# A group's first products copied by ScalarE, and VectorE's residuals put one behind each of those products

## The reference

```python
x = layer_norm(DEEPNORM_ALPHA * x + g1 * mix, ln1_g, ln1_b)
h2 = x * (1.0 + sc2) + sh2
f = jnp.einsum("btf,fd->btd", jnp.square(jax.nn.relu(jnp.einsum("btd,df->btf", h2, w_up))), w_down)
x = layer_norm(DEEPNORM_ALPHA * x + g2 * f, ln2_g, ln2_b)
```

## Time and profile before

| | |
|---|---|
| median of 3 runs (lowest, highest) | 2214.82 us (2210.22 to 2215.65) |
| the profiled execution | 2205.87 us, its span 2204.2 us |
| mean granted TensorE clock | 0.986 |
| PE busy | 2110.0 us, 96% |
| DVE busy | 1513.3 us, 69% |
| POOL busy | 1461.9 us, 66% |
| ACT busy | 863.2 us, 39% |

### The profile page before, as it was taken

One profiled execution on the slowest core, in us unless ns is written; L12 is line 12 of the kernel. 1 busy time (PEld: TensorE's weight loads), 2 busy tenths in 40 slices (PEclk: granted clock), 3 DMA queues, 4 the chain that ended last, 5 costly groups with the idle time before them and its releaser, 6 DMA issues.

```text
span 2204.2 us, 27806 instructions
## 1 busy us (share of the span) xinstructions
PE 2110.0 (96%) x10342; PEld 1741.9 (79%) x10342; DVE 1513.3 (69%) x2055; ACT 863.2 (39%) x1173; POOL 1461.9 (66%) x1115
## 2 busy tenths in 40 slices
PE   7989999999989999999989999999999999999994
PEld 3556788788889788888868888877888889999983
DVE  1554479778687665567788757698857787665578
ACT  1200322323212355445544545644554554444440
POOL 4324578786424367787787778877878876666675
PEclk9999999999999999999999999999999999999997
DMA  8546588795333254454624564534564544444331
GB/s 265 159 153 219 200 240 254 211 279 178 113 105 116 86 187 146 159 185 135 200 94 145 177 217 144 173 111 143 182 212 145 168 121 125 146 166 151 116 125 43
DMA packets 324089, 357.78 MB, mean 162 GB/s; under 512 B 16280, under 2 KB 256105, under 8 KB 323954
## 3 DMA queue, kind: packets, MB, share of 16 engines
q1 hardware_dynamic: 323954, 355.99, 51.1%
HBM read 321.34 MB, written 34.59 MB: 161 GB/s over the span
## 4 chain that ended last, share of the span: by engine, by line
PE 64%; DVE 12%; issue 1%; ACT 1%; DVEq 0%; ACTq 0%
PE ps L1096 21%; PE ps L1097 20%; PE ps L1098 20%; PE ps L1361 1%; DVE xt L1922 1%; DVE hid_a L1880 1%; DVE pair_sums L1900 0%; DVE pair_sums L1899 0%; DVE pair_sums L1901 0%; DVE hid_b L1880 0%; PE ps L1430 0%; DVE mix L1541 0%; DVE more_sums L1985 0%; DVE acc L1990 0%; DVE htmp L1723 0%
## 5 line engine op out<-in xcount | busy, mean ns | idle before, releaser
L856 POOL TENSOR_TENSOR w_hilo<-w_raw,w_hilo 128x512 fp32r<-128x512 f32 x890 | 1279.5, 1467 | 692.5 <-ACT w_hilo L941 692.2
L941 ACT ACTIVATE w_hilo<-w_raw 128x1024 fp32r<-128x1024 f32 x445 | 470.6, 1059 | 712.8 <-PE ps L1098 606.4
L1096 PE MATMUL ps<-hA,w_hilo 128*128 128x512 f32 (+1 forms) x1760 | 622.2, 354 | 16.1 <-ACT htmp L992 8.0
L1097 PE MATMUL ps<-hA,w_hilo 128*128 128x512 f32 (+1 forms) x1760 | 620.8, 353 | 0.0
L1098 PE MATMUL ps<-hA,w_hilo 128*128 128x512 f32 (+1 forms) x1760 | 620.3, 352 | 0.0
L1096 PEld LDWEIGHTS ps<-hA,w_hilo 128*128 128x128 f32 x1760 | 332.2, 189 | 60.1 <-issue 15.4
L1097 PEld LDWEIGHTS ps<-hA,w_hilo 128*128 128x128 f32 x1760 | 332.2, 189 | 41.6
L1098 PEld LDWEIGHTS ps<-hA,w_hilo 128*128 128x128 f32 x1760 | 332.1, 189 | 41.7
L1972 DVE TENSOR_TENSOR acc<-acc,ps 128x512 f32<-128x512 f32 x270 | 178.4, 686 | 78.0 <-PE ps L1098 75.1
L1096 PE MATMUL ps<-w_hilo,hid_a 128*128 128x512 f32 x450 | 178.0, 396 | 7.3 <-DVE more_sums L1969 7.3
L1096 PE MATMUL ps<-w_hilo,hid_b 128*128 128x512 f32 x450 | 175.5, 390 | 3.5 <-POOL w_hilo L856 3.5
(11 more groups left out here) (233 smaller groups left out, 3014.9 us busy)
## 6 DMA issues: line engine op xcount, KB each, us to landing
w_raw<-in_w_up SPq DMA_DIRECT2D x128, 512.0 KB, 4.0
w_raw<-w_mix SPq DMA_DIRECT2D x124, 512.0 KB, 3.3
w_raw<-in_w_down SPq DMA_DIRECT2D x97, 512.0 KB, 3.6
w_raw<-in_w_in SPq DMA_DIRECT2D x64, 512.0 KB, 4.7
xt<-in_w_ada SPq DMA_DIRECT2D x22, 1024.0 KB
w_raw<-in_w_out SPq DMA_DIRECT2D x32, 512.0 KB, 5.0
xt<-x_norm SPq DMA_DIRECT2D x19, 512.0 KB, 5.7
xt<-in_w_down SPq DMA_DIRECT2D x36, 256.0 KB, 5.1
```

Source lines behind the costliest of these rows:

```text
L856: ins = pool.tensor_tensor(W[:, g % SLOTS, 1, cols], raw[:, g % RAW, cols], W[:, g % SLOTS, 0, cols], ALU.subtract)
L941: act.activation(W[:, g % SLOTS, 0, :], raw[:, g % RAW, :], ACT.Copy).then_inc(hi_done, 1)
L1096: pe.matmul(out, w_hi, x_hi, start=start, stop=False)
L1097: pe.matmul(out, w_hi, x_lo, start=False, stop=False)
```

## The change

ScalarE copies a group's seven first products into the places of the sums (`begin_sums`), in all four groups. For the groups behind the first it waits until the old contents are no longer needed: `sums_ready` for the places of products 0 to 2, and a new semaphore `x_added`, which each residual raises, for those of products 3 to 6. The copies stand ahead of the `hi_part` of the same product. VectorE copies nothing there any more. Its residuals of tiles 3, 2, 1, 0 stand behind K(b,0), K(b,1), K(b,2), K(b,3), one each. The statistics of tiles 3 and 2 stay behind K(b,4); those of tiles 1 and 0 and the inverse root move behind K(b,6).

```diff
+            def begin_sums(b, j):
+                s = b // BLOCKS
+                if s:
+                    act.wait_ge(d_evac, 2 * PRODUCTS * b)
+                    act.wait_ge(sums_ready, 2 * s - (1 if j < 2 else 0))
+                    if j > 2:
+                        act.wait_ge(x_added, 4 * s - (2 if j < 5 else 0))
+                for i in range(2):
+                    if i:
+                        act.wait_ge(slab_used, SLAB["K", b, j] + 1)
+                    else:
+                        act.wait_ge(d_done, PRODUCTS * b + j + 1)
+                    act.activation(sums_of[j](i), ps[:, product_bank(b, j, i), :], ACT.Copy).then_inc(d_evac, 1)
...
+                if kind == "K" and b % BLOCKS == 0:
+                    begin_sums(b, i)
...
-                do(dve.scalar_tensor_tensor(x, x, ALPHA, acc[0:r, t, :], ALU.mult, ALU.add))
+                signal(dve.scalar_tensor_tensor(x, x, ALPHA, acc[0:r, t, :], ALU.mult, ALU.add), x_added,
+                       4 * s + 4 - t)
...
-                    if b % BLOCKS == 0:
-                        dve.tensor_copy(a, src).then_inc(d_evac, 1)
-                    else:
-                        dve.wait_ge(d_evac, sums_done(b - 1, j, i))
-                        dve.tensor_tensor(a, a, src, ALU.add).then_inc(d_evac, 1)
+                    dve.wait_ge(d_evac, sums_done(b - 1, j, i))
+                    dve.tensor_tensor(a, a, src, ALU.add).then_inc(d_evac, 1)
...
-                elif i == 2:
-                    end_residual(s, 3)
-                    end_residual(s, 2)
...
-                if s and r == 1 and n == 0:
-                    for t in range(4):
+                if s and r == 1:
+                    for t in ((3, 2), (1, 0))[n]:
                         end_sums(t)
-                    sync()
-                    rsqrt(0, 4, ln_end)
+                    if n:
+                        sync()
+                        rsqrt(0, 4, ln_end)
...
-                else:
+                elif b % BLOCKS:
                     down(b, i)
...
-                if (kind, i) == ("K", 1) and s and r == 0:
-                    end_residual(s - 1, 1)
-                    end_residual(s - 1, 0)
+                if kind == "K" and i < 4 and s and r == 0:
+                    end_residual(s - 1, 3 - i)
```

More of the change, by code:

```diff
@@ L464, in decoder_layer_kernel @@
         acc_gated = sem("acc_gated")
+        x_added = sem("x_added")
         y_scaled = sem("y_scaled")
```

## The result

The changed kernel takes 2197.82 us (median of 4 runs, 2192.95 to 2199.85), the kernel before beside it 2214.28 (4 runs). The ratio is 0.9925, 95% interval 0.9904 to 0.9947. Timed again with more runs, it took 2194.3 against 2212.3 us, ratio 0.9918 (0.9904 to 0.9931). So the change is faster by 0.5 to 1.0%. The profiled execution took 2192.95 us, with a span of 2191.1 and a mean clock of 0.987.

The account below looks back on a forecast made before the run. PE, busy 96% of the span, bounds the kernel, so only its holes and slow-clock stretches can give time. Gains of 6.5 us in group 1 and 7.6 in group 2, 14.1 together, take 2214.8 to 2200.7 us; range 2193 to 2209.

Parts of the forecast that it names:

- No hole before U(9,2): Start of groups 1 and 2: earlier pair sums remove PE's 3.99 us wait and the slow clock behind it.
- the clock rival: New wait before K(8,3), K(16,3) also lowers the clock; 1.7 + 2.4 us come back, 2204.8 us; chance 0.17.
- The way from the pair sums to K(8,3): Group 1: from the end of (9, first pair)'s sums through ScalarE's copy to K(8,3)'s start, 4.8 us.
- When the pair sums of (9, first pair) end: VectorE, group 1: at 1137.4, with 0.97 us of GpSimd contention for each of three low parts.
- my 3.2: Predicted new PE wait before K(8,3) for ScalarE's copy of K(8,1), 3.2 us in place of 0.70.
- No wait behind it: After K(8,3): K(8,4) follows at once, later copy waits are covered and slab parts cost nothing.
- the likeliest case: The forecast itself: 2200.7 us, own range 2197 to 2204, chance 0.55.
- the rival of slab parts behind every copy: All 28 first products: PE waits 2 × 0.60 us each, losing 33.4 us, time 2234.1 us; chance 0.06.
- ScalarE waiting for a residual without PE: Copies of K(8,3) wait on ScalarE for two residuals until about 1145.7, covered to within a few tenths.
- ScalarE's busy time: Profile after the change: ScalarE 33 us busier, from 14 copies a group at 0.60 us.
- Groups 0 and 3 and the statistics at nothing: Copies in groups 0 and 3, and moving the statistics and inverse root of tiles 1 and 0, change nothing.
- The clock: Group 3's 3.24 us hole left the clock at 1.00, taken as evidence against the new 3.2 us hole lowering it.

Follow-up runs that it names:

- Experiment 3: Changed kernel with the residuals of tiles 3 and 2 put back behind U(8,2) and U(16,2): 2200.0 us, ratio 0.9952 to the kernel before.
- experiment 8: Both kernels profiled again, nothing edited: the kernel before took 2207.35, 2209.65 and 2213.6 us, the changed kernel 2195.73 us.
- Experiment 7: Changed kernel with K(8,4)'s slab high part early and ScalarE's copies of K(8,1), K(16,1) ahead of it: 2193.65 us, ratio 0.9915 to the kernel before.
- The third trace: Third profiled execution of the changed kernel, nothing edited: 2195.73 us.
- The second execution: Second profiled execution of the changed kernel, nothing edited; the kernel timed again had a median of 2194.3 us, ratio 0.9918 to the kernel before.
- experiment 6: Changed kernel with the high part of K(8,4)'s slab ahead of the pair sums' high parts, groups 1 and 2: 2193.67 us, ratio 0.992 to the kernel before.
- experiment 2: Changed kernel with residuals and statistics at their old places, so only the copies on ScalarE remain: 2201.91 us, ratio 0.9961 to the kernel before.
- experiment 4: Changed kernel with all statistics and the inverse root back behind K(8,4): 2197.39 us, ratio 0.9946 to the kernel before.
- experiment 5: Changed kernel with ScalarE copying in groups 1 and 2 only, VectorE in groups 0 and 3: 2197.03 us, ratio 0.9934 to the kernel before.

## Why the prediction was right, step by step

Predicted were 2200.7 us, 14.1 us less; measured were 2197.82 and 2194.3, with differences of 16.5 and 18.0.

**No hole before U(9,2): right.** I had the pair sums end 0.17 us after K(8,0)'s start (1125.6 against 1125.43) and found 0.18, and the clock is 1.00 behind it. Experiment 3 brings the hole back with the residuals alone. The clock behind the hole was no loss by itself, as experiment 8 shows; my sum did not count it, since it went by the start of K(8,4), but the clock rival took its price of 1.7 and 2.4 us from there.

**The way from the pair sums to K(8,3): right.** I took 4.8 us; it is 1139.67 − 1134.89 = 4.78 in group 1 and 4.77 in group 2. Experiment 7 removes that wait by taking the copies out of this chain.

**When the pair sums of (9, first pair) end: mis-sized by up to 1.4 us.** I took 11.8 us behind those before them, with 0.97 of contention for each of three low parts. It is 10.4 in group 1 and 11.6 in group 2. The first low part takes 2.29 or 2.30 in place of 1.23, the 128x512 one stays at 0.69, and the third is the one that varies. VectorE in group 2, and GpSimd there:

```profile
1462.13 1.57 DVE L1898 TENSOR_TENSOR hid_a<-htmp,hid_a 128x256 fp32r<-128x256 f32 x1
```

```profile
1462.12 8.47 POOL L857 TENSOR_TENSOR w_hilo<-w_raw,w_hilo 128x512 fp32r<-128x512 f32 x6 [1.83 <-ACT w_hilo L942]
```

Where GpSimd's slab part started 0.01 us ahead (1462.12), the low part took 1.57 us; where both started at 1128.72, it took 0.42. The third trace has the same pair, 1.57 and 0.42, and the hole before K(8,3) follows: 2.77 and 2.75, against 1.61 and 1.62. The second execution, for which I had expected one of these two sizes, shows a third in group 1: the part of `outputs` took 1.22 us, the sums before it ended 1.15 us earlier, and the three low parts took 2.29, 1.67 and 1.41, which is all of my contention; the hole is 2.43. So that hole has several sizes, 1.6 to 2.8 us, and none as long as my 3.2.

**No wait behind it: wrong.** I had costed the slab parts at nothing in the likeliest case and gave PE no hole before U(9,3). There is one of 0.63 to 0.99 us in each group where the clock stayed up. Its cause is not the rival of slab parts behind every copy (whose price of 28 × 1.20 is 33.6 us, not 33.4). It is the one `hi_part` behind the pair sums' high parts, and a GpSimd slowed beside the residuals; experiment 6, which moves that instruction, removes it. The limit is not new: the kernel before had it, hidden under the wait for the copies of K(8,2) (experiment 2). It takes back what K(8,3) gained on my figure. I had K(8,3) 16.8 us behind K(8,0), and it came 15.4 to 16.5 behind; I had 10.9 us from there to K(8,5), and it took 12.2 to 12.6. So that my K(8,5), 19.5 + 2.72 + 5.44 = 27.7 us behind K(8,0), is close to the six measured distances, 27.60 to 29.10, is partly luck: two errors of opposite sign.

**ScalarE waiting for a residual without PE: right.** It idled 2.43 us in group 1, and no hole of PE ends there. **ScalarE's busy time** rose by 26.2 us, not 33: two copies back to back take 1.06 us together.

**Groups 0 and 3 and the statistics at nothing: right** by the traces of experiments 4 and 5.

**The clock: read from one execution, and wrong as a rule.** I said that a hole of 3.24 us leaves the clock at 1.00. The same hole, released by the same instruction, stands in all fourteen profiled executions of the nine kernels, 3.23 or 3.24 us long. The way from its end to K(24,0) took 19.14 to 19.16 us in four, 20.47 to 20.71 in nine and 21.96 in one. So the clock rival was not excluded by the row that I set against it; it came true in one of six holes of the changed kernel, and cost 0.3 us there, not the 1.7 or 2.4 that I had set for it. Of the four that kept the clock three are of the kernel before, so the change may lose about 1.2 us there; why, is open. In return the hole before K(8,4), which I priced at its 2.7 us, cost 1.4 to 1.6 us of clock in five of eight places, and that goes too. The advice in the Trainium skill ("TensorE: Matmul & The Clock Gate", section "Why this matters for your kernels") against idle gaps agrees with this. Here the clock fell also behind gaps shorter than the one I had taken as safe and shorter than those of which the Trainium skill warns: 2.17 us in experiment 6.

**The sum.** By the mean distances the change is worth (35.6 + 36.0) − (28.4 + 28.4) = 14.8 us (three executions of the changed kernel), less 1.2 in group 3: 13.6. The mean spans differ by 2207.4 − 2194.3 = 13.1 us; the rest is 0.7 us by which the changed executions reach K(8,0) later on average, and 0.2 us less behind K(24,0). The timed difference of 18.0 has an interval of 15.3 to 21.2 us, so at least 1.7 us of it are not explained (the first timing's, 11.7 to 21.3, holds the 13.6). The executions differ by up to 6.3 us in when they reach K(8,0) (1123.79 to 1130.11). All of that lies ahead of the MLP, which the change leaves alone: from K(0,0) to K(8,0) is the same in each. Whether the unexplained rest is there stays open.

## What to carry to other kernels

When holes of the bottleneck engine are the target, take several profiled executions first: here one trace showed a hole of 3.99 us that is 2.85 in others, and a clock that held where it mostly falls. A stretch at the lower clock ahead of another wait may cost nothing, because the wait takes it up; price it by the start of the product behind that wait. A hole that is removed uncovers the one under it: here the supply of slabs, no later than before. Look for the one instruction of the supply chain that stands behind a wait, and put it ahead (experiments 6 and 7). A copy that another engine waits for should not stand behind a chain that waits for a third.

## What the runs showed of the hardware

**A tie between VectorE and GpSimd.** The same 128x256 low part takes 0.42 us or 1.57, and the same 128x1024 addition 1.22 or 2.35, and which it is goes by GpSimd's start. At the starts of groups 1 and 2 the fourteen traces, which hold the starts in ns, have 52 of these low parts and additions that begin within 0.03 us of an instruction with which GpSimd leaves an idle stretch. In 38 of them GpSimd's start lies 5 to 24 ns ahead, and VectorE's instruction took 1.1 us longer. In the other 14 it lies at most 4 ns ahead, or later than VectorE's, and VectorE's took no longer. The Trainium skill ("SBUF — State Buffer", section "SBUF: two separate sides") describes the pair of ports that they share as an exclusive lock, which whoever starts first holds for the whole instruction. The traces agree but for those 4 ns, and some 0.01 us decided over 1.15 us of PE's time.

**The clock behind equal holes.** Holes of 2.85 us in one execution left the clock at 1.00 and at 0.78; holes of 2.43 to 2.78 us left it at 1.00 in five places of the changed kernel and experiment 5, at 0.76 in three of the changed kernel and experiment 4; behind holes of 3.97 to 3.99 us the next 24 matmuls took 1.4 us or more longer in all seven places with one. The shortest hole of groups 1 and 2 behind which it fell is the 2.17 us of experiment 6. What beside the length of the hole decides, no run here shows.

**What a lower clock costs.** Behind the holes of 2.85 to 3.99 us in the kernel before it cost nothing, since a wait for VectorE followed; behind the changed kernel's new hole 0.3 us, since a wait for a slab went with it; behind the hole of 2.7 us before K(8,4), and in experiment 6, 1.4 to 1.6 us, since nothing followed that could take it up.
